# One decoder block on eight cores: the first 32-bit products of k are made from scaled activations, and the shift is added from products of one column

## The reference, cut to what matters

```python
mod = silu(c) @ w_ada + b_ada                     # six parts of 1024 per sequence
shift1, scale1, gate1, shift2, scale2, gate2 = split(mod, 6)
h = rmsnorm(x, norm1_w) * (1 + scale1) + shift1
p = h @ w_in                                      # q, k, v, g, lr, cb, cc, cx, ga, gb
log_a = log_sigmoid(lr @ w_gate_up + b_gate) / 16
b = cumsum(log_a within a chunk)
q_dec = q * exp(b);  k_dec = k * exp(-b)
o = gated linear attention of q_dec, k_dec, v with a running state
...
x = x + gate1 * (merge of o and of a short convolution) @ w_out
x = x + gate2 * squared_relu_mlp(rmsnorm(x) modulated by shift2, scale2)
out = rmsnorm(x) * final_norm_w
```

## Time and profile before

| | |
|---|---|
| median of 3 runs | 1268.44 us (1268.21 to 1269.2) |
| the profiled execution: its own time, its span | 1268.44 us, 1266.9 us |
| span of the even cores 0, 2, 4, 6 | 1266.9, 1264.7, 1266.5, 1265.6 us |
| span of the odd cores 1, 3, 5, 7 | 1246.0, 1247.0, 1244.1, 1243.5 us |
| PE busy on core 0 | 1222.1 us, 96% of the span |
| DVE, ACT, POOL busy | 721.5, 432.1, 96.4 us |
| granted PE clock, mean of core 0 | 0.993 of full speed |

### The profile page before, as it was taken

One profiled execution on the slowest core, in us unless ns is written; L12 is line 12 of the kernel. 1 busy time (PEld: TensorE's weight loads), 2 busy tenths in 40 slices (PEclk: granted clock), 3 DMA queues, 4 the chain that ended last, 5 costly groups with the idle time before them and its releaser, 6 DMA issues.

```text
span 1266.9 us, 20151 instructions; the slowest of 8 cores (1243.5 to 1266.9 us)
## 1 busy us (share of the span) xinstructions
PE 1222.1 (96%) x7050; PEld 660.6 (52%) x7149; DVE 721.5 (57%) x1206; ACT 432.1 (34%) x981; POOL 96.4 (8%) x150
## 2 busy tenths in 40 slices
PE   3899999999999999999999999999999999999996
PEld 2665665555555555555555545555445545544553
DVE  3467876666666543333233476766656656654766
ACT  3487876431111332111111255411121121123553
POOL 3004343200000000000000000000000000000000
PEclk9899999999999999999999999999999999999998
DMA  8930101535346312112222900032120330033222
GB/s 224 243 105 2 51 2 34 117 63 109 63 79 102 70 34 35 34 34 38 44 48 44 311 2 1 12 73 53 29 53 1 67 67 1 1 67 68 85 113 88
DMA packets 16026, 84.42 MB, mean 67 GB/s; under 512 B 2112, under 2 KB 2208, under 8 KB 10288
## 3 DMA queue, kind: packets, MB, share of 16 engines
q0 software_dynamic: 8784, 58.76, 23.4%
q1 hardware_dynamic: 6992, 24.03, 5.1%
q10 hardware_dynamic: 144, 0.26, 0.1%
HBM read 124.40 MB, written 8.91 MB: 105 GB/s over the span
## 4 chain that ended last, share of the span: by engine, by line
PE 92%; DMA 3%; issue 2%; ACT 1%; DVE 1%; POOL 0%; POOLq 0%; DVEq 0%; ACTq 0%
PE psf L489 90%; DMA wsl_a<-w_ada 3%; PE psf L499 2%; ACT hT_a L475 0%; ACT Bt_a L434 0%; DVE Bt_a L482 0%; POOL xb_a L572 0%; DVE h32T_a L444 0%; DVE x_a L456 0%; ACT tmp_a L475 0%; DVE x_a L441 0%; POOL wsl_a L535 0%; ACT tmp_a L434 0%; POOLq L1555 0%; DVE tmp_a L441 0%
## 5 line engine op out<-in xcount | busy, mean ns | idle before, releaser
L489 PE MATMUL psf<-hT_a,wsl_a 128*128 128x384 bf16 (+1 forms) x3461 | 660.1, 346 | 3.7 <-POOL S_bf_a L450 1.1
L489 PEld LDWEIGHTS psf<-hT_a,wsl_a 128*128 128x128 bf16 x3488 | 339.8, 98 | 296.2 <-issue 2.9
L434 ACT ACTIVATE tmp_a<-psf 128x512 f32<-128x512 f32 (+1 forms) x280 | 149.1, 533 | 530.5 <-PE psf L489 518.1
L489 PE MATMUL psf<-wsl_a,aT_a 128*128 128x512 bf16 x1071 | 235.0, 377 | 1.3
L489 PEld LDWEIGHTS psf<-wsl_a,aT_a 128*128 128x128 bf16 x1096 | 107.2, 98 | 126.2
L441 DVE TENSOR_TENSOR tmp_a<-tmp_a,psf 128x384 f32<-128x384 f32 (+1 forms) x80 | 48.7, 608 | 158.6 <-ACT tmp_a L434 158.6
L441 DVE TENSOR_TENSOR aT_a<-tmp_a 128x384 bf16<-128x384 f32 (+1 forms) x128 | 78.6, 617 | 96.1 <-ACT tmp_a L434 94.6
L441 DVE TENSOR_TENSOR x_a<-x_a,tmp_a 128x512 f32<-128x512 f32 x171 | 117.7, 689 | 18.4 <-DVE tmp_a L441 3.5
L441 DVE TENSOR_TENSOR tmp_a<-psf,g2b_a 128x512 f32<-128x512 f32 (+1 forms) x137 | 94.1, 687 | 59.6 <-PE psf L489 58.8
L450 POOL TENSOR_SCALAR S_bf_a<-S_a,dec 128x256 bf16<-128x256 f32 x64 | 58.5, 932 | 126.6 <-DVE S_a L456 126.5
L489 PE MATMUL psf<-cbuT_a,wsl_a 128*128 128x384 bf16 (+1 forms) x313 | 65.0, 346 | 0.4
(11 more groups left out here) (157 smaller groups left out, 902.3 us busy)
## 6 DMA issues: line engine op xcount, KB each, us to landing
wsl_a<-w POOLq DMA_DIRECT2D x16, 1024.0 KB, 9.6
wsl_a<-w_ada POOLq DMA_DIRECT2D x12, 1024.0 KB, 12.5
x_a<-x_cur SPq DMA_DIRECT2D x17, 512.0 KB, 6.4
wsl_a<-w_merge POOLq DMA_DIRECT2D x8, 1024.0 KB, 8.9
out<-x_a SPq DMA_DIRECT2D x16, 512.0 KB, 2.6
wsl_a<-w_conv POOLq DMA_DIRECT2D x8, 768.0 KB, 7.0
xb_a<-x_cur SPq DMA_DIRECT2D x9, 512.0 KB, 4.6
xb_a<-x_cur POOLq DMA_DIRECT2D x8, 512.0 KB, 19.9
```

The costliest lines, as they stand in the source:

```text
L434: P.op("act", lambda e: e.activation(out=out, in_=in_, func=func, **kw), r, w, cost=0.19 + 0.00083 * size(in_) + (0.2 if "accum_out" in kw ...
L489: ins = e.matmul(out=o, lhsT=l, rhs=rh, start=st, stop=sp_)
```

## The change

The transposes of `xn32` move ahead of the shift: `special_front` is now called before the k products and no longer needs the shift. Its results, scaled by `a1T` alone, go into a new tile `h32s` (four chunks by ACT, four by DVE). The 32-bit products of k for the first 128 tokens are made from `h32s` and stand in the list right behind `ada(0)` and `ada(1)`. The shift's part of k for these tokens is a new group of 32 products, stationary `w32k`, moving one 32-bit column of `modT`, which DVE copies to `ks`; two DVE operations for each head now add `ks` while they multiply by the decay. `h32T`, still needed for q, is made in `special_shift` by eight DVE additions of `modT` to `h32s`.

```diff
@@ -381,6 +381,7 @@
             MT = B("MT", [8, 512], BF16, oA + 24 * KB)
             h32T = B("h32T", [8, 128], F32, oA + 8 * KB)
             hTs = B("hTs", [8, 512], BF16, oA + 16 * KB)
+            h32s = B("h32s", [8, 128], F32, oA + 24 * KB)
             junk = B("junk", [1024], BF16, oA + 12 * KB)
             ogT = [B(f"ogT{t.i}", [8, t.w], BF16, oB + t.s0 * 4 * KB) for t in main]
             cbuT = [B(f"cbuT{t.i}", [8, t.w], BF16, oB + (t.s0 * 4 + t.n * 2) * KB) for t in main]
@@ -840,11 +841,19 @@
                 for half in range(2):
                     p_, pk, _ = bank()
                     TR([(p_[:, j * 128:(j + 1) * 128], xn32.t[:, (half * 4 + j) * 128:(half * 4 + j + 1) * 128]) for j in range(4)],
-                       xn32.k() + identf.k() + SH, pk, idn=identf.t)
+                       xn32.k() + identf.k(), pk, idn=identf.t)
                     for j in range(4):
                         kc = half * 4 + j
-                        Vts(h32T.t[:, kc, :], p_[:, j * 128:(j + 1) * 128], a1T[:, kc:kc + 1], modT[:, kc:kc + 1],
-                            ALU.mult, ALU.add, pk + ["a1T", ("modT", 0), ("modT", 4)], h32T.k((kc * 128, 128)))
+                        o, i_, rd, wr = h32s.t[:, kc, :], p_[:, j * 128:(j + 1) * 128], pk + ["a1T"], h32s.k((kc * 128, 128))
+                        if half:
+                            Vsmul(o, i_, a1T[:, kc:kc + 1], rd, wr)
+                        else:
+                            A(o, i_, AF.Copy, rd, wr, scale=a1T[:, kc:kc + 1])
+
+            def special_shift():
+                for kc in range(8):
+                    Vsadd(h32T.t[:, kc, :], h32s.t[:, kc, :], modT[:, kc:kc + 1], h32s.k((kc * 128, 128)) + SH,
+                          h32T.k((kc * 128, 128)))
 
             def run(ps):
                 for _, f in ps:
@@ -896,10 +905,16 @@
             wkk = [wkk]
             if first:
                 wkk = cast("k")
+            if first:
+                special_front()
             k0 = [k_mm(hs, h, 128 if first else 0, T0.w) for h in range(4)]
             ada(0)
             ada(1)
             if first:
+                for h in range(4):
+                    p_, pk = k0[h]
+                    MM([(p_[:, 0:128], w32k.t[:, kc, h * 128:(h + 1) * 128], h32s.t[:, kc, :], kc == 0, kc == 7)
+                        for kc in range(8)], w32k.k() + h32s.k() + pk, pk)
                 done_w(4)
                 xload(seq[1], eng="pool")
             else:
@@ -910,11 +925,16 @@
                + [(p_[:, h:h + 1], wk_[:, kc, h * 128:(h + 1) * 128], sh_bf[:, kc:kc + 1], kc == 0, kc == 7)
                   for h in range(4) for kc in range(8)], ["wlr", "shbf"] + wkk, pk)
             Vcopy(shb[:, 0:5], p_[:, 0:5], pk, ["ce"])
+            if first:
+                p_, pk, _ = bank()
+                MM([(p_[:, h:h + 1], w32k.t[:, kc, h * 128:(h + 1) * 128], modT[:, kc:kc + 1], kc == 0, kc == 7)
+                    for h in range(4) for kc in range(8)], w32k.k() + SH, pk)
+                Vcopy(ks[:, 0:4], p_[:, 0:4], pk, ["ks"])
             run([lr_piece(T0, lr0)])
             run(gate_pieces(T0))
             if first:
-                special_front()
                 run([tr_piece(T0, kc) for kc in range(8)])
+                special_shift()
             else:
                 for j in range(2):
                     t_, tk = tmp()
@@ -988,11 +1008,10 @@
                         Vtt(kd.t[:, h, 0:w], p_[:, 0:w], e2[:, 0:w], ALU.mult, pk + e2k, kd.k((h * 512, w)))
                         return
                     p_, pk = k0[h]
-                    hs = slice(h * 128, (h + 1) * 128)
-                    MM([(p_[:, 0:128], w32k.t[:, kc, hs], h32T.t[:, kc, :], kc == 0, kc == 7) for kc in range(8)],
-                       w32k.k() + h32T.k() + pk, pk)
-                    Vtt(kd32.t[:, h, :], p_[:, 0:128], e2[:, 0:128], ALU.mult, pk + e2k, kd32.k((h * 128, 128)))
-                    Vtt(kd.t[:, h, 0:128], p_[:, 0:128], e2[:, 0:128], ALU.mult, pk + e2k, kd.k((h * 512, 128)))
+                    Vstt(kd32.t[:, h, :], p_[:, 0:128], ks[:, h:h + 1], e2[:, 0:128], ALU.add, ALU.mult, pk + e2k + ["ks"],
+                         kd32.k((h * 128, 128)))
+                    Vstt(kd.t[:, h, 0:128], p_[:, 0:128], ks[:, h:h + 1], e2[:, 0:128], ALU.add, ALU.mult, pk + e2k + ["ks"],
+                         kd.k((h * 512, 128)))
                     Vstt(kd.t[:, h, 128:w], p_[:, 128:w], shb[:, h:h + 1], e2[:, 128:w], ALU.add, ALU.mult,
                          pk + e2k + ["ce"], kd.k((h * 512 + 128, w - 128)))
                 return (1.73, f)
```

## The result

The changed kernel takes 1280.86 us, the median of 4 runs (1280.55 to 1283.07), against 1268.53 us for the kernel before beside it (4 runs): a ratio of 1.0097, with a 95% interval from 1.0084 to 1.011. The forecast was 1280.8. The profiled execution of the changed kernel is the longest of the four, 1283.07 us, with a span of 1281.5; the even cores of the other three end at 1277.7 to 1279.5. In some executions one die runs at a lower clock and takes some per cent longer; the medians of the experiments are of all executions, the ratios leave such executions out, and without its one `e_hold_clock` has a median of 1285.72 us.

A forecast was written before the change was run, and what follows sets the result against it. The even cores' heads were taken as the bound: the first q products on the slowest even core move from 61.6 to 74, and these 12.4 us on 1268.44 give 1280.8 us, range 1271 to 1285.

The forecast's parts named there:

- Ahead of `ada(2)`: Head on PE: eight 32-bit transposes, then 12 fillers, make ada(3) start at 27.4, 2.6 us later; bounds 1.9 and 4.
- Up to the k products: From ada(3) through hTs, scaling and casts on ACT and DVE: bf16 k products start at 34.75, 2.05 us later.
- The products that move: 24 32-bit k products take 5.5 us where fillers and a wait stood; ada(1) starts at 46.25, 3.5 late.
- The group: 32 one-column w32k products, 64 instructions at 0.11 us, 0.22 once the clock falls at 51.4: from 49.95 to 62.6.
- From its end to q: Gate chain on DVE and ACT takes 10.9 us behind the one-column products, to 73.5; 21 fillers end at 74.5.
- The rest: From the first q products to the end of the span: unchanged, 1205 us, with all lateness at q arriving at the end.
- Cheap products: Rival: one-column w32k products take 1.6 us in all, q at 62.5, 1269.3 us, or 1270.5 with low-clock fillers; chance 0.13.
- Clock stays up: Rival: full clock through the one-column w32k products, which end at 57.0; q at 67.9, 6.3 us late, 1274.7; chance 0.18.
- Faster: Rival: PE's own work limits shift to q; balance 5.8 us less the one-column products' cost, 1264.2 to 1265.9; chance 0.07.

The follow-up runs named there:

- e_hold_clock: Changed kernel plus a 512-column filler product behind every second one-column product of w32k, 16 in all: 1286.6 us, ratio 1.0127 to the kernel before.
- e_rows_gate: Changed kernel with the w32k group behind the gate's products, no 12 fillers ahead of ada(2), and swapped operands (modT column stationary, w32k moving): 1274.92 us, ratio 1.0047.
- e_hold32: Changed kernel plus a 512-column filler product behind each of the 32 one-column products of w32k: 1281.17 us, ratio 1.0095 to the kernel before.
- e_no_head_fill: Changed kernel without the 12 fillers ahead of ada(2): 1279.1 us, ratio 1.008 to the kernel before.
- e_bf_cols: Changed kernel with the 32 one-column products made from bf16 weights and the bf16 shift: 1270.28 us, ratio 1.0009 to the kernel before.

## Why the prediction was right

The step that decided it, one-column products of 32-bit weights at the pace of full ones, held: 0.11 us for each of 64 instructions at the full clock, and the clock falling among them. Point by point (M is the end of the group):

- *Ahead of `ada(2)`.* `ada(3)` was forecast for 27.4 and started at 26.62 to 28.59. The clock rose sooner on core 2 and later on core 0, where the 12 fillers took 4.85 us. The bounds (1.9 to 4 us late) held.
- *Up to the k products.* Forecast 34.75, measured 33.90 to 35.87.
- *The products that move.* `ada(1)` forecast 46.25, measured 45.34 to 47.31, without a wait, as forecast; 48 instructions took 5.44 (5.5).
- *The group.* Forecast from 49.95 to 62.6, the clock falling at 51.4 with 13 of 64 instructions done. On core 4 it began at 49.69 and the clock fell at 51.44 (0.68 in the window from 50 is 1.44 us at full clock), with 16 done at 0.109; the other 48 took 0.215 each and not 0.22, and the end was 61.74. On core 2 the clock fell at 50.5, on core 0 at 54; the cores that start the group later keep the clock longer, so the ends lie within 0.5 us.
- *From its end to q.* The chain to the last cast of `w32q` was forecast at M + 10.9 and measured at 73.55 - 61.74 = 11.8. The last logarithm was forecast at M + 8.5 and ended at 71.27, M + 9.5: ACT had five `hT` chunks ahead of the gate (3.46 us) where four were counted. The 21 fillers ended at 74.8 (74.5), and it is they that q followed, 1.3 us behind the cast. One sum of the prediction does not come out: for a fall of the clock at 52.8 its own terms give a group's end at 61.2 and a cast at 72.1, and not 72.8; the forecast does not rest on it.
- *The rest.* Forecast 1205.3 behind q; it was 1206.6 on cores 0, 2 and 4 of the profiled execution. These 1.3 us were not foreseen (last section): the prediction had read the time behind q as free of waits that change. The profiled execution so comes to 74.84 + 1206.6 = 1281.4, with 1.6 around the span 1283.0, which is 2.2 above the median; that the median fell on the forecast within 0.1 us is luck, since the terms were off by up to 1.3 us.
- *The rivals.* Cheap products: ruled out by the trace; the bf16 group shows what cheap ones would have given (forecast 1269.3 to 1270.5, measured 1270.28). Clock stays up: it did on no even core; the core of e_hold_clock that kept it ended 5.7 to 7.6 us ahead of the others of the same execution, with 16 fillers in the group, where 6.1 were forecast without fillers. Faster: it supposed that PE's own work limits what lies between shift and q. With the group at 0.8 us and the 12 fillers gone, the result is 1.0001 (0.9991 to 1.001). Taking the k products and transposes from there shortened it by 0.9 to 2.9 us, where the rival had counted on 11.2 less the group, and the later start took that back; the chain over DVE and ACT then sets q, and PE waits 1.6 to 3.3 us for it as soon as fillers don't fill the gap.

So the loss of 12.3 us is, by kernels with the same queues, 10.6 for the group (with what waits for it, and its clock) and 1.8 for the late head (11.2 and 2.2 by the ratios). The two are not independent: leaving the fillers out is worth 1.8 us with the 32-bit group and 1.0 with the bf16 one (1270.28 and 1269.25). With both undone the moved products remain, and their balance is nothing that can be measured.

## What to carry to other kernels

Here a product of one column cost what its weights cost to load: with 32-bit weights of 128 columns that was as much as 128 moving columns (0.109 against 0.113 us an instruction), so splitting a shift off a 32-bit product of 128 columns doubles it. Before moving a product away from a stretch, see what ends the stretch; here a chain of DVE and ACT was close behind PE's own work, the moved work had been lying largely beside it, and what the split added stood ahead of it. An experiment that lets a planner reorder the rest measures the reordering too: fix the queues, or compare where the time went behind the edit.

## What the runs showed of the hardware beyond that

PE that the profile shows as 100% busy can lose its clock. In the changed kernel PE and PEld were busy for 4.00 of 4.00 us in the windows shown and the granted clock still went to 0.50; 16 fillers of 512 columns inside the group kept the clock on one core of four, 32 on all. And the clock is lost again by single waits late in the program. Core 0 of the changed kernel, profiled execution:

```profile
248.71 3.54 PE L490 MATMUL psf<-hT_a,wsl_a 128*128 128x512 bf16 x8 [1.65 <-DVE S_a L457]
...
248.00:252.00 4.00, 3.29 (x8) 1.17 (x9) 3.98 (x15) 0.72 (x3) 3.89 (x5) 0.58 1.06 221
```

Before, the same products waited 1.12 us at 234.0 and ran at the full clock. Now they wait 1.65, and eight of them take 3.54 us where core 6 needs 1.89, after a wait of 1.84: of four cores with waits of 1.6 to 2 us, three lost the clock, and in e_hold_clock again three of four (waits of 1.65 to 2.10). A wait of 1.42 lost it on core 0 of e_rows_gate at 176 and not on core 2; one of 1.61 at 206 in the kernel before did not. Kernels with the same queues do without this wait: e_hold32, e_no_head_fill and e_bf_cols wait 1.10 us or less at this place, keep the clock, and need 1204.0 to 1205.2 us from q to the end on every even core, where the changed kernel needs 1206.6 on the three cores that lost it and 1205.1 on core 6. Why the wait grew is not settled; in the kernels with bf16 columns it is 0.7 to 1.4 us. PE's pace ahead of it relative to the transfer of `w_conv` may be the reason, which no run shows.
